# Latent attention in an 8-bank PSUM pipeline: the values of a half as one run of six key tiles instead of three runs of two

## The reference

```python
def one(qblk):
    s = jnp.einsum('bqhd,bkhd->bhqk', qblk, k, preferred_element_type=jnp.float32) * scale
    p = jax.nn.softmax(s, axis=-1).astype(v.dtype)
    return jnp.einsum('bhqk,bkhv->bqhv', p, v)
...
yx = _attend_blocks(q_x, k_all, v_all) @ mla_w_o[j]
```

## Time and profile before

| | |
|---|---|
| median of 3 runs | 3264.24 us (3261.81 to 3265.47) |
| the profiled execution, its own time | 3265.15 us |
| its span | 3263.3 us |
| TensorE busy in the span | 3193.4 us (98%) |
| VectorE, ScalarE, GpSimd busy | 1624.1, 1301.2, 1332.4 us |
| mean granted TensorE clock | 0.992 of 2.4 GHz |
| the latent items | from 1002.6 us (first scores) to 1261.34 us (last values) |

### The profile page before, as it was taken

How to read it: one execution, slowest core, us unless ns; L and a number is a source line. 1 busy time by engine, 2 the same in 40 slices (tenths; PEclk the granted TensorE clock), 3 DMA queues, 4 the chain that set the end, 5 groups by cost and what they waited for, 6 DMA issues and landing times.

```text
span 3263.3 us, 40240 instructions
## 1 busy us (share of the span) xinstructions
PE 3193.4 (98%) x16204; PEld 2558.9 (78%) x16204; DVE 1624.1 (50%) x2703; ACT 1301.2 (40%) x2307; POOL 1332.4 (41%) x754
## 2 busy tenths in 40 slices
PE   7999999999998999999999999999999999999998
PEld 4876888888875557888886888888887788878886
DVE  5877376322337773432324686253432668445252
ACT  4323431222345665432334445343333544444243
POOL 2222423232253445444452234644455234464445
PEclk9999999999999999999999999999999999999999
DMA  7323334112132001423232120423333111222321
GB/s 272 105 94 126 116 110 145 56 61 67 54 120 89 14 14 47 148 81 116 72 125 84 46 62 19 147 92 96 100 88 116 52 65 49 58 95 78 116 80 56
DMA packets 85926, 288.17 MB, mean 88 GB/s; under 512 B 9803, under 2 KB 10379, under 8 KB 84972
## 3 DMA queue, kind: packets, MB, share of 16 engines
q1 hardware_dynamic: 85740, 285.60, 26.6%
HBM read 283.47 MB, written 2.10 MB: 88 GB/s over the span
## 4 chain that ended last, share of the span: by engine, by line
PE 89%; DVE 5%; issue 1%; ACT 1%; POOL 1%; DMA 1%; SPq 0%; POOLq 0%; DVEq 0%; ACTq 0%
PE ps L504 20%; PE ps L507 20%; PE ps L505 20%; PE ps L563 2%; PE ps L565 2%; PE ps L564 2%; PE ps L2131 2%; PE ps L2980 1%; PE ps L2201 1%; PE ps L1371 1%; PE ps L2571 1%; PE ps L483 1%; PE ps L478 1%; PE ps L522 1%; PE ps L479 1%
## 5 line engine op out<-in xcount | busy, mean ns | idle before, releaser
L452 POOL TENSOR_TENSOR WL<-ring,WH 128x1024 fp32r<-128x1024 f32 (+2 forms) x427 | 926.7, 2173 | 1398.4 <-ACT WH L441 1398.0
L504 PE MATMUL ps<-HX,WH 128*128 128x512 f32 x1656 | 649.7, 392 | 0.0
L507 PE MATMUL ps<-HX,WL 128*128 128x512 f32 x1656 | 648.4, 392 | 0.0
L505 PE MATMUL ps<-HX,WH 128*128 128x512 f32 x1656 | 646.8, 391 | 0.0
L441 ACT CAST WH<-ring 128x1024 fp32r<-128x1024 f32 (+2 forms) x443 | 421.2, 951 | 529.5 <-PE ps L507 471.2
L504 PE MATMUL ps<-FR,WH 128*128 128x512 f32 x1120 | 419.2, 374 | 0.3
L505 PE MATMUL ps<-FR,WH 128*128 128x512 f32 x1120 | 410.0, 373 | 0.0
L507 PE MATMUL ps<-FR,WL 128*128 128x512 f32 x1120 | 389.7, 374 | 0.0
L504 PEld LDWEIGHTS ps<-HX,WH 128*128 128x128 f32 x1656 | 311.3, 188 | 67.5 <-issue 0.8
L507 PEld LDWEIGHTS ps<-HX,WL 128*128 128x128 f32 x1656 | 312.4, 189 | 44.8
L505 PEld LDWEIGHTS ps<-HX,WH 128*128 128x128 f32 x1656 | 311.4, 188 | 44.7
(11 more groups left out here) (400 smaller groups left out, 5331.9 us busy)
## 6 DMA issues: line engine op xcount, KB each, us to landing
ring<-in_ffn_w_up SPq DMA_DIRECT2D x88, 512.0 KB, 3.4
ring<-in_w_up SPq DMA_DIRECT2D x88, 512.0 KB, 3.3
ring<-in_w_mod SPq DMA_DIRECT2D x64, 512.0 KB, 4.1
ring<-in_w_in_tok SPq DMA_DIRECT2D x40, 512.0 KB, 3.5
ring<-in_w_mod_columns SPq DMA_DIRECT2D x32, 512.0 KB, 4.4
ring<-in_w_in_feat SPq DMA_DIRECT2D x32, 512.0 KB, 3.3
ring<-in_ffn_w_down SPq DMA_DIRECT2D x32, 384.0 KB, 3.1
ring<-in_w_out SPq DMA_DIRECT2D x32, 384.0 KB, 3.1
```

Of the source, the lines that this page charges most:

```text
L452: pool.tensor_tensor(WL[:, p % SPLITS, 0:n], ring.ap(r), WH[:, p % SPLITS, 0:n], ALU.subtract).then_inc(*ring.frees(r, split.g, "low", p))
L504: pe.matmul(o, high, xh, first, False)
L505: pe.matmul(o, high, xl, False, False)
L507: m = pe.matmul(PS[bs[i]][:, 0:N], low, get(k)[0], False, last)
```

## The change

The three pieces of a half become one run of all six key tiles (24 passes in the profile). It stands in step 4v+8, one step later than the first piece did and one step earlier than the last. The copy of the bank moves from step 4v+10 to step 4v+9. The loop has 72 steps instead of 71. The release of the score banks and the two early key tiles of the output projection go with the first piece, so they move from steps 63 and 67 to 64 and 68. VectorE's subtraction for halves 12 and 13 moves from step 62 to 61. No instruction is added or removed.

```diff
-        def lat_values_pe(pe, v, part):
+        def lat_values_pe(pe, v):
             n, q = v // 4, v // 2
             c0 = v % 2 * 256
-            if part == 0 and v % 2 == 0:
+            if v % 2 == 0:
                 bank.hold("lv", q)
                 pe.wait_ge(*bank.free("lv", q))
-            if part == 0:
-                pe.wait_ge(*att.a.at("turned", 4 * v + 3, 1))
+            pe.wait_ge(*att.a.at("turned", 4 * v + 3, 1))
             o = ps("lv", q)
-            for j in range(2 * part, 2 * part + 2):
+            for j in range(6):
                 for x in range(2):
                     c = (q % 2 * 2 + x) * 64
                     m = pe.matmul(o[64 * x:64 * x + 64, c0:c0 + 256], VT[n % 2][:, j, c:c + 64], PT[x][:, j, c0:c0 + 256],
                                   j == 0, j == 5)
-            if part == 2:
-                m.then_inc(*att.pe.up("values", v))
+            m.then_inc(*att.pe.up("values", v))
 
         def lat_values_a(act, v, part):
-            if part < 3 or v % 2 == 0:
+            if part != 1 or v % 2 == 0:
                 return
...
-            for i in range(71):
+            for i in range(72):
...
-                if i >= 7:
-                    values(*divmod(i - 7, 4))
+                if i >= 8:
+                    values(*divmod(i - 8, 4))
...
-                if v < 16 and part < 3:
-                    lat_values_pe(pe, v, part)
+                if v < 16 and part == 0:
+                    lat_values_pe(pe, v)
...
-                if part == 3 and v in (13, 15):
+                if part == 1 and v in (13, 15):
                     lat_low_v(dve, v // 2)
```

## The result

The changed kernel takes 3278.57 us (median of 4 runs, 3275.55 to 3280.22) against 3264.34 in runs beside it: a ratio of 1.0045 [1.003, 1.006], 14.2 us slower. The forecast was 3268. The time lies at the upper end of the range, on the side of rival B, but as will be seen the clock made up only about a third of the loss. The profiled execution takes 3280.22 us with a span of 3278.4.

The account below looks back on a forecast made before the run. TensorE, busy 98% of the span, was taken as the bound, with VectorE pacing places 4 to 10. Terms -4.0 + 4.1 + 2.8 + 1.0 = +3.9 us on 3265.15 gave 3269.0, 3268 as median; range 3259 to 3279.

Parts of the forecast that it names:

- rival B: Clock falls deeper: runs at places 8 and 12 wholly at half clock, 3284 us, or 3274 to 3278 with one; chance 0.24.
- Term 1: Places 11 to 1, where TensorE sets the pace: two runs replace six pieces, gaining 1.33 us three times, -4.0 us.
- Term 2: Run at place 8, where VectorE sets the pace: late scores delay item 41's maximum 1.37 us, three times, +4.1 us.
- Term 3: Added TensorE idle before item 40's second scores brings half clock near place 8: 1.4 us in two groups, +2.8 us.
- Term 4: Last group and drain: item 60 starts 2.1 to 2.6 us earlier, the drain gives it back, net +1.0 us.
- D: TensorE's saving counts everywhere, VectorE absorbing late scores at place 8: 3254 us, or 3259 with half; chance 0.08.
- E: Nothing moves, because the pieces were hidden in gaps either way: 3264 us; chance 0.03.
- A sign set down for "wrong": A period of the groups not within 68.3 + 1.6 us would show the forecast wrong.

Follow-up runs that it names:

- busy: All halves as runs plus extra unread matmuls at places 6, 7, 9, 10, 11 of three groups, against the kernel before: 3273.76 us, ratio 1.0024.
- busypieces: The kernel before, pieces kept, plus four extra unread matmuls at place 10 of each group with side work: 3260.94 us, ratio 0.9991.
- allruns: The changed kernel's instruction streams again, all sixteen halves as runs, against the kernel before: 3281.52 us, ratio 1.0049.
- busylate2: All halves as runs, copy back at step 4v+10, extra unread matmuls at places 7, 9, 10, 11, against the kernel before: 3267.52 us, ratio 1.0013.
- run0: The kernel before with runs only for halves 2, 6 and 10 (place 0), all others pieces: 3265.33 us, ratio 0.9999.
- runlast: The kernel before with runs only for halves 11, 12 and 13 (steps 52, 56, 60), copies early: 3268.24 us, ratio 1.0009.
- lastlate: The kernel before with runs only for halves 11, 12 and 13, copies and VectorE's subtraction at step 4v+10: 3265.57 us, ratio 1.0005.
- rundrain: The kernel before with runs only for halves 14 and 15 in the drain (steps 64 and 68): 3265.63 us, ratio 1.0002.
- mixedbusy: The kernel before with runs only for halves 2, 6, 10, 11, 12, their copies late, and extra matmuls at place 10: 3260.96 us, ratio 0.9989.

## Why the prediction was wrong, step by step

| term | predicted | measured | from |
|---|---|---|---|
| 1, TensorE stretches | -4.0 | +4.3 | busy against busypieces: 2 x 1.32 + 1.64 |
| 2, run at place 8 | +4.1 | +3.1 | the same: 1.04 + 1.02 + 1.07 |
| 3, clock | +2.8 | +3.6 | 7.8 (allruns to busy) less 4.2 (before to busypieces) |
| 4, last group and drain | +1.0 | +3.6 | busy against busypieces, from item 51's maximum: 49.74 for 46.13 us |
| sum | +3.9 | +14.6 | the whole change: 14.2 measured, allruns 17.1 |

Terms 1, 2 and 4 are distances in two traces at full clock, but for the half clock in the drain of busy, 1.3 us of term 4; term 3 is a difference of medians. With the 1.3 the clock has 4.9 of the 14.6 us. The medians of busy and busypieces, each against the kernel before beside it, lie 13.5 us apart, the three terms come to 11.0; in the two traces 1.7 us more stand before the first maximum and behind the last values, where the streams are the same.

**Term 1 failed, and in its sign; it is 8.3 of the 10.7 us missed.** The step that failed is "the pieces at places 11, 12, 13, 15, 0 and 1 lie on the path": taking pieces away gives back far less than they cost. Item by item in the first two groups, at full clock (busy against busypieces):

| us in a group | predicted | measured |
|---|---|---|
| run for the piece at place 12 | +1.73, and +0.75 of half clock | +1.59 |
| run for the piece at place 0 | +1.73 | +1.73 |
| piece at place 11 gone | -1.91 | 0.00 (item 43 to 44: 3.65 with and without) |
| piece at place 13 gone | -1.21 | -0.15 (4.04 for 4.19) |
| piece at place 15 gone | -1.21 | -0.63 (3.56 for 4.19) |
| piece at place 1 gone | -1.21 | -1.22 (4.53 for 5.75) |
| sum | -1.33 | +1.32 |

In the third group the piece at place 1 was worth only 1.00, and the sum is +1.64.

The two runs cost about what was said. Two things were wrong. First, the chain of the earlier trace rows shows the piece of item 43 on TensorE at half clock, and I counted its 1.91 us as a price that the change would spare; but VectorE was just behind, and even at half clock that piece shows only 0.21 us in the maxima (3.86 for 3.65). A chain says what was last in one execution; how close the next engine was behind it stands in no chain. Second, the steps that lost their piece at places 13 and 15 run into waits of TensorE's transposes instead, 1.0 us at place 14 and 0.5 at place 0, so most of the saving is lost. Half a microsecond of the first is ScalarE's copy. At place 14 the second scores stand 2.52 us behind the first in busy, 2.03 with the copy late (busylate2) and 1.52 in busypieces. I had costed the copy at nothing: the text said "covered by its idle time, 2 us before exponentials at VectorE's pace". That holds where VectorE sets the pace, but at place 13 TensorE does, the steps without pieces are only 3.05 us long there, and ScalarE has no such idle time. With the copy late the stretches are 0.47 us shorter each (29.03 to 28.56). The step to item 48 stays at 3.56 us with the copy at either step, and also in run0, which has its runs at place 0 alone.

Between 0.85 us (28.56 against 27.71) and 1.17 (23.93 against 22.76) a group remain with the copy late: two runs that cost 1.59 and 1.73 more than the pieces they stand for, against three pieces that give back 0, 0.63 and 0.63 and one that gives back 1.0 to 1.2. Nearly all of it comes with the run at place 12. run0, whose first and third groups are at full clock there, has 27.59 us from item 12 to 19 and 22.97 from 44 to 51, for 27.71 and 22.76 in busypieces: a run at place 0 alone changes next to nothing.

The price of a piece was mis-read too. The 1.95 us between transposes in the earlier trace rows is one uneven interval; the next, to 1216.80, is 3.37. By the maxima a step of the last group takes 3.16 us with a piece and 2.16 without, so a piece costs 1.00 us there and not 1.21, and a run 2.73 (4.89 less 2.16). The saving is 0.27 us for a half even where TensorE sets the pace, near the prediction's own lower bound of 0.29, not 0.69.

**Term 2 was right.** The mechanism (the scores of item 41 come late behind the run, VectorE waits) is shown by the maxima 4.03 us apart for 3.02, and the size at full clock is 1.0 a group for 1.37, in all kernels with the run at place 8. "Nothing gives it back before place 11" held.

**Term 3 was right in its direction and short in its size.** I expected a fall at place 8 and took it for 1.4 us in two groups; in the profiled execution it is there in the first two groups (0.57 in both rows) and costs 1.7 each (5.71 us from item 8 to 9 and from 24 to 25, for 4.03). Not foreseen: at place 12 the half clock lasts longer in the changed kernel and meets a run: 4.78 us for 2.74. The term had been net of half a run there (0.75). Nor was the half clock in the drain foreseen, 1.3 us. And over half of the clock's price in the groups, 4.2 of 7.8 us, is one that the kernel before also paid; of that the prediction saw only the piece at place 11. The Trainium skill (TensorE: Matmul & The Clock Gate, HAM oscillation) says that each burst after a wait starts cold; the case that it gives waits for DMA, not for another engine. Here it holds in some groups and not in others: at place 8 the clock is 0.57, 0.57 and 1.00, at place 12 0.52 in the third group, and the run there in the second is at full clock, 2.74 us. The rule gave 7.2 us for place 8 alone; the changed kernel's trace has 3.4 there.

**Term 4 had the place right and the mechanism half.** The two subtractions in step 61 were named, and so was the wait for the cast, but their delay was followed only through TensorE's stream. The chain shows it goes on through item 62's maxima to POOL's scaling and to the transposes, and TensorE, having waited, then runs at half clock: 4.3 us in the drain (23.33 for 19.06), of which 3.6 go with the late copy (to 19.76). runlast, with the subtractions early and no half clock there, has 21.94, so 2.1 us are the wait (to lastlate's 19.84). The early start of item 60 was 0.8 us (26.27 for 27.05), not 2.1 to 2.6. Seven pieces there were worth 7.0 us, not 8.5, and the steps without values take up to 2.59 us instead of 2.16; the chain of the changed kernel goes over ScalarE in those steps, by the copies of line 2185 and the casts of line 2218. TensorE's own order in the drain, which the prediction worked out at length, costs nothing measurable: rundrain is 19.01 us from item 60 on, for 19.06 before, and its ratio is 1.0002.

**The rivals.** B had the side right and its two places right (a run of 4.78 us at place 12, 0.57 at place 8), but not the account: of 14.6 us the clock has 4.9 net, with the drain. That the median, 3278.57, is inside the range of 3259 to 3279 is luck: it is near what was given for B with one place (3274 to 3278), and comes from another sum. D and E were wrong: little of TensorE's saving came through. A sign set down for "wrong" did come: the distance from item 12 to item 28 is 72.3 us, outside 68.3 + 1.6 (the next is 69.0). What lacked among the rivals was one on ScalarE's order, although the change moves ScalarE's copy and its place stood in the text.

**What stays open.** What makes the 0.5 us before the second scores at places 14 and 0 that stay with the copy late was not followed. The clock's phase differs from one execution to another: the changed kernel and allruns have half clock at different places in their traces, and no run here says what decides it. A kernel with only ScalarE's copy late, and VectorE's subtraction where the change puts it, wasn't tried, so the two have their share of the drain's 3.6 us together.

**A faster version.** mixedbusy (runs only where TensorE has no VectorE to wait for, late copies, twelve extra matmuls) takes 3260.96 us, ratio 0.9989 [0.9981, 0.9998], 4.2 us less than before. busypieces has the same 3260.94 with no run at all, so what is won is the clock's; the runs add nothing that can be measured.

## What to carry to other kernels

Work gathered into one burst is paid in full where it lands, while the pieces that it replaces may have cost nothing, or leave a wait where they stood: before counting pieces as saved, ask how far behind the next engine was, not only who is on the chain. Read a price from several intervals that close on each other, not from one. With a moved block, its followers on the other engines (a copy, a subtraction) move too; each is to be costed in the queue that it enters, at the shortest steps of the loop, and may be put back where it stood (here 5.8 of 17 us). Where an engine idles in the middle of a stretch and the windows show its clock falling, try work without use there: the test costs a few lines and tells the clock's share apart from all else.

## What the runs showed of the hardware

More work on TensorE made the kernel faster: 30 extra matmuls took 7.8 us off allruns (3281.52 to 3273.76), 12 took 4.2 us off the kernel before (3265.14 to 3260.94), with the granted clock of the third group at 1.00 where it had been 0.93 and 0.95. The extra matmuls stood in steps where TensorE waited for VectorE and cost no time of their own: the stretches with place 8 are 40.0 us in busy, as they are in allruns where its clock is full (40.03, 39.98). In the kernel before, TensorE idles where it is hidden behind VectorE, and the price is taken afterwards, at places 11 and 12, when it comes back onto the path at half clock (item 43 to 44 3.86 us for 3.65, item 44 to 45 4.19 for 2.84).
